# A mixture-of-experts kernel: expert block codes read without range tests, and the second expert product as three fp32r products

## The reference

```python
# moe(xt, router_w, router_bias, w1, w3, w2, sw1, sw3, sw2), cut
scores = sigmoid(xt @ router_w)                      # 64 experts
_, idx = top_k(where(emask, scores + bias, -1e30), 8)  # 8 experts a token, from 4 of 8 groups
# tokens sorted by expert, each expert padded to blocks of 128 slots
def expert_block(tok, e):
    xb = xpad[tok]                                   # 128 x 1024
    h = silu(xb @ w1[e]) * (xb @ w3[e])              # 128 x 256
    return h @ w2[e]                                 # 128 x 1024
routed = zeros.at[slot_tok].add(yb * slot_w)
```

## Time and profile before

| what | value |
|---|---|
| time, median of 3 runs | 2918.18 us (2916.14 to 2931.74) |
| profiled execution, span from first to last instruction | 2922.5 us |
| mean granted TensorE clock, share of full | 0.950 |
| PE matmul busy | 2607.3 us, 89% of the span |
| PEld weight loads busy | 1616.5 us, 55% |
| DVE busy | 1659.2 us, 57% |
| ACT busy | 1308.7 us, 45% |
| POOL busy | 510.7 us, 17% |

### The profile page before, as it was taken

How to read it: one execution, slowest core, us unless ns; L and a number is a source line. 1 busy time by engine, 2 the same in 40 slices (tenths; PEclk the granted TensorE clock), 3 DMA queues, 4 the chain that set the end, 5 groups by cost and what they waited for, 6 DMA issues and landing times. The chain is left out here.

```text
span 2922.5 us, 50877 instructions
## 1 busy us (share of the span) xinstructions
PE 2607.3 (89%) x11129; PEld 1616.5 (55%) x11130; DVE 1659.2 (57%) x3062; ACT 1308.7 (45%) x2097; POOL 510.7 (17%) x662
## 2 busy tenths in 40 slices
PE   7998999968999999999949998988799999999980
PEld 3434545446666666666614446744566666666650
DVE  3335643555656665665548308925566766765646
ACT  3115642145555554555513205621456655654641
POOL 0000000122222222222200000000222322222222
PEclk9998999989999999999979998999899999999995
DMA  6772012078978977877776201012789878887767
GB/s 257 292 280 61 1 64 74 34 282 304 343 266 306 348 276 254 299 273 254 257 291 245 94 0 61 1 55 81 280 300 330 325 292 309 323 307 257 294 220 295
DMA packets 143559, 649.00 MB, mean 222 GB/s; under 512 B 33936, under 2 KB 41104, under 8 KB 85500
## 3 DMA queue, kind: packets, MB, share of 16 engines
q1 hardware_dynamic: 80412, 423.94, 39.0%
q10 hardware_dynamic: 19552, 137.45, 13.1%
q0 software_dynamic: 43520, 86.68, 8.1%
HBM read 627.94 MB, written 91.31 MB: 246 GB/s over the span
## 5 line engine op out<-in xcount | busy, mean ns | idle before, releaser
L1953 PE MATMUL e_psH<-e_w13h,e_xh 128*128 x1184 | 594.5, 502 | 65.1 <-issue 37.4
L2136 DVE TENSOR_TENSOR e_w13l<-ring,e_w13h x512 | 592.5, 1219 | 81.2 <-ACT e_w13h L2041 78.3
L1979 PE MATMUL e_psY<-ring,e_gt 128*128 x1184 | 566.5, 606 | 5.1 <-ACT e_gt L2054 5.1
L2041 ACT CAST e_w13h<-ring x512 | 497.8, 1043 | 136.6 <-DMA ring<-in_exp_w 81.1
L1953 PE MATMUL e_psH<-e_w13l,e_xh 128*128 x1184 | 474.9, 401 | 0.0
L2149 DVE TENSOR_TENSOR e_xl<-e_psT,e_xh 128x512 fp32r<-128x512 f32 x296 | 196.6, 688 | 402.2 <-issue 201.1
L1939 PE MATMUL e_psT<-ident,e_xg 128*128 128x128 f32 x1184 | 324.6, 277 | 10.1 <-DMA e_xg<-h_rows,e_gidx 6.2
L1953 PEld LDWEIGHTS e_psH<-e_w13h,e_xh 128*128 128x128 f32 x1184 | 228.7, 193 | 181.6 <-issue 145.5
L1959 PE MATMUL e_psH<-e_w13h,e_xl 128*128 x1184 | 307.9, 402 | 0.0
L1979 PEld LDWEIGHTS e_psY<-ring,e_gt 128*128 128x128 f32 x1184 | 213.9, 190 | 163.5 <-issue 151.1
L2061 ACT CAST e_xh<-e_psT 128x512 fp32r<-128x512 f32 x296 | 169.7, 588 | 257.9 <-PE e_psT L1939 134.3
(11 more groups left out here) (297 smaller groups left out, 2875.8 us busy)
## 6 DMA issues: line engine op xcount, KB each, us to landing
ring<-in_exp_w SPq DMA_DIRECT2D x256, 1024.0 KB
ring<-in_exp_w ACTq DMA_DIRECT2D x130, 1024.0 KB
p_lead<-in_ada_w SPq DMA_DIRECT2D x44, 1024.0 KB, 6.4
v<-y_rows SPq DMA_DIRECT2D x54, 512.0 KB, 5.5
f_Y<-y_rows SPq DMA_DIRECT2D x12, 1536.0 KB, 12.7
ring<-in_c_w_in SPq DMA_DIRECT2D x6, 2048.0 KB, 12.4
ring<-in_sh_w SPq DMA_DIRECT2D x6, 1024.0 KB
h_rows<-r_hrow SPq DMA_DIRECT2D x10, 512.0 KB, 2.6
```

Of the source, the lines that this page charges most:

```text
L1953: nc.tensor.matmul(psH[par][:], xh[par][:, k * P:(k + 1) * P], w[:, bass.DynSlice(half, 1), :, k, :], start=(k == 0 and i == 0), stop=False)
L1979: mm = nc.tensor.matmul(psY[:, c * 512:(c + 1) * 512], gt[par][:, k * P:(k + 1) * P], raw2[:, bass.DynSlice(half, 1), k, c * 512:(c + 1) * ...
L2041: nc.scalar.copy(w13h[:, bass.DynSlice(half, 1), :, k, :].rearrange("p o u k n -> p (o u) (k n)"), raw13[:, bass.DynSlice(half, 1), :, k, ...
L2136: nc.vector.tensor_tensor(low, raw, high.bitcast(F32), ALU.subtract).then_inc(w13_lo, 1)
```

## The change

Four edits, all in `experts`.

1. `codes` reads the block codes without the range test that followed each of them. TensorE's `down` no longer needs the code of its own block, so TensorE reads six codes for a pair of blocks instead of seven.
2. ScalarE gets `split2`: for every block, the two halves (k = 0, 1) of w2 of its expert, 128x1024 each, are copied to the fp32r tile `e_w2h`. The gate copy writes the fp32r tile `e_gth`.
3. VectorE gets `rest2` (two subtractions of 128x1024 to `e_w2l`) and `gate` (one subtraction of 128x256, psG minus `e_gth`, to `e_gtl`) at the end of each block's step.
4. TensorE's `down` is gate_high w2_high + gate_high w2_low for each k, and then gate_low w2_high: 12 fp32r matmuls of 128x512 instead of 4 fp32 ones. `turn_gate` of a block waits until the gate_low of the block before has been made, since both use psG.

```diff
@@ codes
-    ... min_val=0, max_val=8 * E * E - 1)[1]
+    ... min_val=0, max_val=8 * E * E - 1, skip_runtime_bounds_check_because="settle clamps every entry")[1]
@@ TensorE
             def turn_gate(b):
                 pe.wait_ge(g_ready, b + 1)
-                wait_for(pe, gt_ready, b)
+                wait_for(pe, gt_lo, b)
...
-            def down(b, par, code, between):
-                o, half = order_in(code), half_in(code)
-                pe.wait_ge(gt_ready, b + 1)
+            def down(b, par, between):
+                pe.wait_ge(gt_hi, b + 1)
                 wait_for(pe, y_ready, b)
-                pe.wait_ge(w2_in, 16 * o + 16)
+                for k in range(KF):
+                    pe.wait_ge(w2_lo, KF * b + k + 1)
+                    for i, w in enumerate((w2h, w2l)):
+                        for c in range(2):
+                            nc.tensor.matmul(psY[:, c * 512:(c + 1) * 512], gth[par][:, k * P:(k + 1) * P], w[:, k, c * 512:(c + 1) * 512],
+                                             start=(k == 0 and i == 0), stop=False)
+                    if k == 0:
+                        between()
+                pe.wait_ge(gt_lo, b + 1)
                 for k in range(KF):
                     for c in range(2):
-                        mm = nc.tensor.matmul(psY[:, c * 512:(c + 1) * 512], gt[par][:, k * P:(k + 1) * P],
-                                              raw2[:, bass.DynSlice(half, 1), k, c * 512:(c + 1) * 512], start=(k == 0), stop=(k == KF - 1))
-                    if k == 0:
-                        between()
+                        mm = nc.tensor.matmul(psY[:, c * 512:(c + 1) * 512], gtl[par][:, k * P:(k + 1) * P],
+                                              w2h[:, k, c * 512:(c + 1) * 512], start=False, stop=(k == KF - 1))
                 mm.then_inc(y_mm, 1)
@@ ScalarE
-                nc.scalar.copy(gt[par][:], psG[:, 0:F]).then_inc(gt_ready, 1)
+                nc.scalar.copy(gth[par][:], psG[:, 0:F]).then_inc(gt_hi, 1)
+            def split2(b, code):
+                act.wait_ge(w2_in, 16 * order_in(code) + 16)
+                act.sem_inc(act_clear, 1)
+                wait_for(act, y_mm, b)
+                for k in range(KF):
+                    nc.scalar.copy(w2h[:, k, :], raw2[:, bass.DynSlice(half_in(code), 1), k, :].rearrange("p o n -> p (o n)")).then_inc(w2_hi, 1)
...
                     rows_out(b - 1, m, 1 - par)
                     next2(b, code)
+                split2(b, code)
                 gate(b, par)
@@ VectorE
+            def rest2(b, code):
+                for k in range(KF):
+                    dve.wait_ge(w2_hi, KF * b + k + 1)
+                    raw = raw2[:, bass.DynSlice(half_in(code), 1), k, :].rearrange("p o n -> p (o n)")
+                    nc.vector.tensor_tensor(w2l[:, k, :], raw, w2h[:, k, :].bitcast(F32), ALU.subtract).then_inc(w2_lo, 1)
+            def gate(b, par):
+                dve.wait_ge(gt_hi, b + 1)
+                nc.vector.tensor_tensor(gtl[par][:], psG[:, 0:F], gth[par][:].bitcast(F32), ALU.subtract).then_inc(gt_lo, 1)
...
                 rest13(b + 2, later)
                 indices(b + 4)
+                rest2(b, code)
+                gate(b, par)
```

More of the change, by code:

```diff
@@ L1816, in experts @@
         ge, g = sb("e_ge", [P, F]), sb("e_g", [P, F])
-        gt = [sb(f"e_gt{i}", [P, F]) for i in range(2)]
+        gth, gtl = ([sb(f"e_gt{n}{i}", [P, F], F32R) for i in range(2)] for n in "hl")
+        w2h, w2l = (sb(f"e_w2{n}", [P, KF, D], F32R) for n in "hl")
         ysb = [sb(f"e_y{i}", [P, D]) for i in range(2)]
@@ L1969, in turn_gate, with step @@
                 tr.then_inc(gt_mm, 1)
-            def down(b, par, code, between):
-                o, half = order_in(code), half_in(code)
-                pe.wait_ge(gt_ready, b + 1)
+            def down(b, par, between):
+                pe.wait_ge(gt_hi, b + 1)
                 wait_for(pe, y_ready, b)
-                pe.wait_ge(w2_in, 16 * o + 16)
+                for k in range(KF):
[7 more added lines that the diff above has]
+                pe.wait_ge(gt_lo, b + 1)
                 for k in range(KF):
                     for c in range(2):
-                        mm = nc.tensor.matmul(psY[:, c * 512:(c + 1) * 512], gt[par][:, k * P:(k + 1) * P],
-                                              raw2[:, bass.DynSlice(half, 1), k, c * 512:(c + 1) * 512], start=(k == 0), stop=(k == KF - 1))
-                    if k == 0:
-                        between()
+                        mm = nc.tensor.matmul(psY[:, c * 512:(c + 1) * 512], gtl[par][:, k * P:(k + 1) * P],
+                                              w2h[:, k, c * 512:(c + 1) * 512], start=False, stop=(k == KF - 1))
                 mm.then_inc(y_mm, 1)
-            def step(b, m, par, before, code, later, first=False):
+            def step(b, m, par, code, later, first=False):
                 def beside(k):
@@ L1995, in step @@
                 else:
-                    down(b - 1, 1 - par, before, lambda: index(b + 4, par, later))
+                    down(b - 1, 1 - par, lambda: index(b + 4, par, later))
             n = pairs(pe)
@@ L2003, in _ @@
                 turn(0, 0, 0, k)
-            step(0, 0, 0, None, code[0], code[4], True)
-            step(1, 1, 1, code[0], code[1], code[5])
+            step(0, 0, 0, code[0], code[4], True)
+            step(1, 1, 1, code[1], code[5])
             with pe.Fori(0, n - 1) as i:
-                code = codes(pe, 2 * i + 1, 7)
-                step(2 * i + 2, i + 1, 0, code[0], code[1], code[5])
-                step(2 * i + 3, i + 2, 1, code[1], code[2], code[6])
+                code = codes(pe, 2 * i + 2, 6)
+                step(2 * i + 2, i + 1, 0, code[0], code[4])
+                step(2 * i + 3, i + 2, 1, code[1], code[5])
             m = ending(pe)
-            code = codes(pe, m + 1, 2)
-            hidden(m + 2, 0, code[1], lambda k: turn_gate(m + 1) if k == 2 else None)
-            down(m + 1, 1, code[0], lambda: None)
+            code = codes(pe, m + 2, 1)
+            hidden(m + 2, 0, code[0], lambda k: turn_gate(m + 1) if k == 2 else None)
+            down(m + 1, 1, lambda: None)
             turn_gate(m + 2)
-            down(m + 2, 0, code[1], lambda: None)
+            down(m + 2, 0, lambda: None)
         @block.scalar
@@ L2099, in _ @@
             next2(m + 2, code[0])
+            split2(m + 2, code[0])
             gate(m + 2, 0)
@@ L2175, in _ @@
             m = ending(dve)
+            code = codes(dve, m + 2, 1)
             product(m + 2, 0)
+            rest2(m + 2, code[0])
+            gate(m + 2, 0)
 def combine(nc, s, a, l, tiles):
```

8 lines of the change are left out of this document (4 added, 4 removed).

## The result

The changed kernel takes 2881.47 us (median of 4 runs, 2875.62 to 2885.97), the kernel before, run on the same chip, 2924.15 (4 runs, 2916.14 to 2931.74). The ratio is 0.9859 with a 95% interval of 0.9829 to 0.9889: 1.4% faster, where the forecast was 2928 us, 9.8 us slower, with a chance of 0.25 on faster.

A forecast was written before the change was run, and what follows sets the result against it. VectorE was to bound the expert phases: 1645 us of steps and loop ends, less 66, plus 12 for late weights and 5 for phase ends, 1596 against 1586.6. Forecast 2918.2 + 9.8 = 2928 us, range 2870 to 2990.

The forecast's parts named there:

- the loop end on VectorE: VectorE's block-code read at each loop end: 4.12 us idle before, 1.94 us left without the tests, 73 times.
- the 66 us for blocks without a new expert: 20 expert-phase blocks leave out the four w13_low subtractions on VectorE: 3.3 us each taken, 66 us off the sum.
- The tests on TensorE: Range tests at TensorE's loop end: had other work beside them, booked at nothing; without that cover under 1 us a pair.
- Late weights: ScalarE's waits for w13, 81.1 us in all: 12 us added, since a slower step hides part of the lateness.
- So 2 us of slack: no wait: VectorE's subtractions in each block: w2_high ready at +6.2 us, wanted at +7.8, so they don't wait for ScalarE.
- VectorE's step: VectorE's full step in a block with a new expert: 7.70 us before, 10.43 us after in the first layer.
- TensorE's own step: TensorE's step in the expert phase, cut by 0.56 us a block through the cheaper second product, to 9.80 us.
- TensorE waiting for w2_low: TensorE stands idle ahead of the second product, waiting for VectorE's w2_low; idle 1.5 us of each 11.27.
- The granted clock: Expert phases: wrong if it fell under 0.9; rival with TensorE at 0.80 some 3070 us, chance 0.04.
- The gain on TensorE is eaten by VectorE: Main case for the expert phases: the bound moves to VectorE, 9.8 us slower, 2928 us, chance 0.50.
- VectorE is cheaper than booked: Rival: code load 1.03 us, blocks without a new expert give their whole 4.34 us; 2868 us, chance 0.20.
- the cheaper product: TensorE's second product: 0.56 us less for each of 148 blocks, 83 us if TensorE stayed the bound, chance 0.04.

The follow-up runs named there:

- Experiment 3: Changed kernel with VectorE's four short index instructions moved after the w2_low and gate_low subtractions: 2979.40 us, ratio to the kernel before 1.0198.
- experiment 4: Changed kernel with one w2_low subtraction a block left out (2866.67 us), half of each w1 and w3 loaded (2834.78 us), or both (2793.92 us).
- two semaphores: Changed kernel with the w1 and w3 loads counted on one semaphore per buffer half: 2843.11 us, ratio to the kernel before 0.9744.
- experiment 2: Changed kernel with the range tests put back, so the split second product alone: 3001.63 us, ratio to the kernel before 1.0283.
- experiment 1: Kernel before with only its range tests taken out, second product still plain fp32: 2892.79 us, ratio 0.9889.
- the mixed split: Changed kernel with only half of w2 split, once an expert, other half plain fp32: 2885.25 us; with a semaphore per buffer half 2804.71 us.
- experiment 8: Weight loads counted on one semaphore per buffer half: changed kernel 2843.11, w2 split once an expert 2861.04, before without range tests 2841.50, half of w2 split 2804.71 us.
- experiment 7: Kernel before with half of w1 and w3 loaded, range tests gone on VectorE alone (2919.82 us) or on TensorE alone (2842.80 us).

## Why the prediction was wrong

**The step that failed** is the loop end on VectorE: "At each loop end VectorE's queue reads the block codes, and nothing covers it", 1.94 us that "stays", 142 us of the sum. All idle time before the 296 x_low instructions is 20 us, of which the releaser is "issue" in 9.7. The rows behind the step were of the kernel before, where the load follows the short index instructions. The change puts 2.7 us of queued work in their place. The order of the instructions was known, with the three long ones directly ahead of the load; the idle time of before was carried over as if it belonged to the load, when it belonged to what stood ahead of it. Experiment 3 shows it: put short instructions ahead of the load, and 1.93 us on average are idle again. The term stands twice in the sum: the 66 us for blocks without a new expert rest on it too ("At least 2 x 11.27 - 2 x 9.80 = 2.9 us"). With 9.7 / 73 = 0.13 us in its place the pair is 20.73 us, 1.1 us above TensorE's 19.6, so 22 us at least and not 66. An estimate by the prediction's own way is then 1504 + 10 - 22 = 1492 us for the phases; with weights on time they measure 1495.5 (experiment 4) and 1496.4 (changed kernel, two semaphores).

The Trainium skill, "Perfetto Trace Analysis", section "Sequencer Loop", says that the sequencer pushes engine instructions into a queue and itself executes control instructions. By that rule, a load behind long queued instructions is covered as far as these last; the traces of experiments 2 and 3 agree: of a load of 1.66 us about 1.0 was covered, of one of 2.12 us nothing.

**The tests on TensorE**, "booked at nothing", "under 1 us a pair": 85 us / 73 = 1.16 us a pair with weights on time. The forecast looked at one loop end, with a step 0.57 us longer than the one beside it. But the phases held 1586.6 - 146 x 10.36 = 74 us above clean steps, 1.0 us a pair, and the row of the sequencer's load and tests on TensorE wasn't read. It isn't a term of the changed kernel's sum, in which VectorE was taken for the bound, but it is what the kernel before lost. TensorE's tests are 85 of the 92 us that all tests cost with half the weights; with all weights the tests together gave 30 of the 43 us (experiment 1), and their shares weren't measured.

**Late weights**, booked at 12 us: half of the bytes are worth 47 us in the changed kernel, two semaphores 38, and in the phases alone 34 and 33. The direction was forecast wrongly too ("A slower step hides part of such lateness"): the step got faster. 1492 + 34 = 1526 us, against 1529.5 measured. This error hides part of the first one: that the time fell inside the range of 2870 to 2990 us is luck, since with weights on time the same kernel takes 2843 us. The other waits change little: "So 2 us of slack: no wait" stands against 77.5 us of waits for w2_high, but VectorE's idle time there lies mostly in the blocks without a new expert, where it has time to spare.

**Right:** VectorE's step (10.43 forecast, 10.49 measured), w2_low at 1.22 us, the matmuls at 0.24 (0.23), TensorE's own step (9.80, 9.72), TensorE waiting for w2_low, and, in part, that VectorE bounds where weights are on time (experiment 4). VectorE's step of 10.5 us in place of TensorE's 10.36 is the likely reason that the product is worth nothing, and the sum said so too; the mixed split, which relieves VectorE, gains 37 us (experiment 8). The granted clock stayed at 0.99. "The gain on TensorE is eaten by VectorE" was right; that the change could be faster for another reason was the rival "VectorE is cheaper than booked", with a chance of 0.20 and 2868 us, and it had the place right but the mechanism wrong: it made the load shorter, where it was covered, and gave the blocks without a new expert their whole 4.34 us.

## What to carry to other kernels

Read idle time at a loop's top together with what is queued ahead of it. Here a register load of 1.3 us behind 2.7 us of subtractions left 0.19 us idle, and one of 2.1 us behind instructions of 0.15 to 0.2 us left 2.63 us; an edit may change which it is. Before crediting a bound engine's own saving, read its sequencer's rows at the loop end; here seven register tests a pair cost TensorE 85 us (with half the weights), as much as the cheaper product was forecast to save it (83). When an edit shows no gain, look whether an input is late because of how it is queued: the mixed split showed nothing against the change until the loads had a semaphore for each buffer half, and then 38 us (2843 to 2805).

## What the runs showed of the hardware that was not expected

- The seven range tests take 2.0 us on TensorE's sequencer (experiment 7) and 1.9 us on VectorE's (experiment 2). The table load took 1698 to 2939 ns on TensorE's in the kernel without VectorE's tests (700 to 1400 us) and 819 to 2125 in the changed kernel (624 to 1400 us); what sets it stays open.
- Half of the weights' bytes brought nothing while TensorE's sequencer was the limit (2927 against 2923), and 58 us once its tests were gone (2893 to 2835).
- A 128x512 fp32r matmul with its own weight load starts 0.23 us after the one before, in the changed kernel's second product too, where the w2 tiles and the halves of psY alternate.
